# Decay matrix from ScalarE, gates straight from PSUM, and the carried state's product scaled in PSUM, in a Mamba-2 and attention block on one core

## The chip, the core and the metric

The kernel runs on one core of a Trainium2 chip. The metric is the device time of one launch, in microseconds (us). The engines are TensorE (PE: matrix products and transposes), VectorE (DVE), ScalarE (ACT: activation functions), GpSimd (POOL) and SyncE (SP, which here only issues the weights' transfers). Each works through its own queue in order, and they wait for each other by semaphores. PSUM is where TensorE writes; SBUF is the main on-chip memory.

## What is computed

A hybrid layer (gated Mamba-2 scan beside dilated attention, then a feed-forward part), followed by two further transformer layers, for 512 tokens of width 1024. The change touches the scan alone:

```python
# 32 heads of 64, 4 groups of 8 heads, state 128, chunks of Q = 128 tokens
a_cs = jnp.cumsum(a, axis=-1)
Lmat = jnp.exp(jnp.where(tri, a_cs[..., :, None] - a_cs[..., None, :], -jnp.inf))
CB = jnp.einsum('bclgn,bcsgn->bcgls', Cr, Br)
y_diag = jnp.einsum('bcgjls,bcsgjp->bclgjp', CB[:, :, :, None] * Lmat, xdt)
...                                     # states carried from chunk to chunk
y_off = jnp.einsum('bclgn,bcgjpn,bcgjl->bclgjp', Cr, prev_states, jnp.exp(a_cs))
y = ssd_chunked(xs, dt, A, Bm, Cm) + d_skip.astype(jnp.float32)[:, None] * xs
y = y.reshape(b, S, SSM_D_INNER) * jax.nn.silu(z.astype(jnp.float32))
# then an RMS norm over each group of 512 channels and the product with w_ssm_out
```

## The kernel before

Every large product is run in float32 as three products of split operands (high x high, low x high, high x low). Weights come in slabs of 256 rows by 256 columns: SyncE fetches them, GpSimd splits them (L563, L565), and TensorE uses them. A panel is 256 output columns, kept in two PSUM banks that two panels share by turns, so a panel can begin once the panel before the last is evicted (semaphore `evicted`).

The scan has 16 units u = 4g + c: group g of 8 heads, chunk c of 128 tokens. The list `SCAN`, written out by hand, fixes one order that every engine follows. Between panels (z: gates, xs: inputs of the next group, "so": output of the group before) it places the steps of the units:

- A(u): TensorE forms the scores of the chunk. VectorE subtracts the columns of the cumulated decay from its rows for 8 heads at once (L1537), takes the minimum with 0 (L1540), forms `xdt` and `xdd`, masks the scores (`cbm`), waits for ScalarE's exponential (L1141) and multiplies it into `M` (L1550). ScalarE then asks for the next unit's decay rows.
- Bp(u): TensorE multiplies `M` by `xdt` (L808), the old state by C (L813) and forms the chunk's addition to the state (L817). VectorE brings `state` up to date (L1558 to L1564) and builds `yb` (L1576 to L1584): skip term, decayed product of the old state (L1578), diagonal part, gate. ScalarE squares `yb` and takes the root (L1156, L1158).
- N(u): VectorE normalizes `yb` to `yn` (L1587, L1592). Cp(u): TensorE transposes `yn` (L822), ScalarE and VectorE split it into `yT_hi` and `yT_lo`.
- epi of a z panel: VectorE scales four blocks out of PSUM into `zbuf` (L1603), ScalarE takes Silu over all of it (L1126).
- xs panels: VectorE scales (cu, L1435) and does three of the four taps of the convolution (L1444), ScalarE the first tap and Silu (`xsf`, L1077), TensorE transposes it (xt, L788).

PSUM bank 0 of `AUX` serves the transposes, bank 1 scores and state, bank 2 the diagonal part, bank 3 the product of the old state.

Of the kernel before, what the change touches and what calls it, by code (L numbers as in the profile page):

```python
# [10 lines left out]
ACT = mybir.ActivationFunctionType  # L11
ALU = mybir.AluOpType
# [240 lines left out]
def build(nc, I, out):  # L253
    ctx = ExitStack()
    with ctx:
# [77 lines left out]
        yoffb = r.put("yoffb", [P, GW])  # L333
# [680 lines left out]
        def _(act):  # L1014
# [96 lines left out]
            def load_decay(u):  # L1111
                g, c = u // NB, u % NB
                load(acs_row[:, u % 2], bass.AP(tensor=acs_dram.tensor, offset=g * HG * S + c * P, ap=[[0, P], [S, HG], [1, P]]), acs_in[u % 2])
# [5 lines left out]
            act.wait_ge(sq_ready, DC)  # L1119
            load_decay(0)  # L1120
            load_gain(0)

            def silu_gate(g, panel):
                act.wait_ge(evicted, 2 * (PAN[("z", g)] + panel) + 2)
                part = zbuf[:, :, panel * PANEL:(panel + 1) * PANEL]
                A(part, part, ACT.Silu).then_inc(z_ready, 1)  # L1126

            def scan_step(tok):
# [9 lines left out]
                elif kind == "A":  # L1138
                    act.wait_ge(acs_in[u % 2], 16 * (u // 2 + 1))
                    act.wait_ge(decay_step, 2 * u + 2)  # L1140
                    A(M[:, u % 2], M[:, u % 2], ACT.Exp).then_inc(decay_exp, 1)  # L1141
                    A(etot[:, u % 2, :], acs_row[:, u % 2, :, P - 1], ACT.Exp).then_inc(decay_exp, 1)
                    if u < 15:
                        if u:
                            act.wait_ge(decay_step, 2 * u)
                            act.wait_ge(decay_exp, 2 * u)
                        load_decay(u + 1)
# [213 lines left out]
        def _(dve):  # L1361
# [154 lines left out]
            def heads(ap):  # L1516
                return ap.rearrange("p (h d) -> p h d", d=HD)
# [6 lines left out]
            def scan_step(tok):  # L1524
# [6 lines left out]
                elif kind == "A":  # L1531

                    dve.wait_ge(acs_in[u % 2], 16 * (u // 2 + 1))
                    if u == 0:
                        dve.wait_ge(tokc_ready, 2)
                    wait(dve, ydiag_done, u - 1)
                    V.tensor_tensor(M[:, u % 2], acs_row[:, u % 2], tokc[:, c, 1, hs].unsqueeze(2).broadcast_to([P, HG, P]),  # L1537
                                    ALU.subtract).then_inc(decay_step, 1)
                    dve.wait_ge(decay_step, 2 * u + 1)
                    V.tensor_scalar(M[:, u % 2], M[:, u % 2], 0.0, None, ALU.min).then_inc(decay_step, 1)  # L1540
# [10 lines left out]
                elif kind == "Bp":  # L1551
# [25 lines left out]
                    if c:  # L1577
                        step(V.tensor_tensor(heads(yoffb[:]), heads(AUX[:, 3, :]), spread(tokc[:, c, 3, hs]), ALU.mult))  # L1578
                    dve.wait_ge(ydiag_done, u + 1)
                    step(V.tensor_tensor(yb[:], yb[:], AUX[:, 2, :], ALU.add))  # L1580
                    if c:
                        step(V.tensor_tensor(yb[:], yb[:], yoffb[:], ALU.add))
                    dve.wait_ge(z_ready, 2 * g + 2)
# [14 lines left out]

            def gate_panel(key, panel):
                done(key, panel)  # L1600
                g = key[1]
                for t in range(NB):
                    ins = V.tensor_scalar(zbuf[:, t, panel * PANEL:(panel + 1) * PANEL], psum_tm(key, panel)[:, t, :], rstd_col[:, t:t + 1], None, ALU.mult)  # L1603
                    if t % 2:
                        ins.then_inc(evicted, 1)
# [49 lines left out]
            for tok in SCAN:  # L1655
                if tok[0] == "epi":
                    key, panel = tok[1], tok[2]
                    if key[0] == "z":
                        gate_panel(key, panel)
                    elif key[0] == "xs":  # L1660
                        conv_panel(key, panel, 8 + 4 * key[1] + 2 * panel)
                    elif key[0] == "so":
                        add_scan_out(key, panel)
                    else:
                        qkv1(key)
                elif tok[0] != "mm":
                    scan_step(tok)
# [389 lines left out]
```

## Time and profile before

| | |
|---|---|
| median of 3 runs | 2751.45 us (2749.63 to 2753.14) |
| the profiled execution's own time | 2752.16 us |
| its span in the profile | 2750.4 us |
| mean granted TensorE clock | 0.969 of full speed |
| TensorE products | busy 2591.3 us (94%) |
| VectorE / ScalarE / GpSimd | busy 1463.7 / 705.3 / 1609.5 us |
| the chain that ended last, by engine | PE 72%, DVE 7%, issue 2%, ACT 1% |

The span is divided by stages in the trace: the scan lies between about 110 and 530 us. A row of a timeline gives the start and the length of an instruction, the engine, the line of the kernel, output <- input, the shape, and in brackets how long the engine had been idle before it and whose work ended that. Idle time of an engine that nobody waits for costs nothing. The granted clock is TensorE's: 1.00 is 2.4 GHz, 0.50 is 1.2 GHz.

### The profile page before, as it was taken

How to read it: one execution, taken by the hardware profiler on the slowest of the kernel's cores; microseconds unless marked ns; L12 is line 12 of the kernel's file. 1: busy time of each engine (PE TensorE's matmuls, PEld its weight loads, DVE VectorE, ACT ScalarE, POOL GpSimd, SP SyncE). 2: the span in 40 equal slices, each digit the busy share in tenths (PEclk: the TensorE clock that was granted, in tenths of full speed). 3: DMA queues.
4: the chain of work that ended last, by engine and by line, in shares of the span. 5: the costliest groups of instructions: out<-in, count | busy, mean ns of one | idle time of the engine just before them, and what ended most of it. 6: DMA issues, size and time to landing. Idle time of an engine off the chain costs nothing.

```text
span 2750.4 us, 37333 instructions
## 1 busy us (share of the span) xinstructions
PE 2591.3 (94%) x12895; PEld 2117.8 (77%) x12895; DVE 1463.7 (53%) x2056; ACT 705.3 (26%) x1251; POOL 1609.5 (59%) x1548
## 2 busy tenths in 40 slices
PE   8889899898999999999999889999999998999998
PEld 6768777787877778888777667888867776788886
DVE  6676676453433533330357757876145445688722
ACT  2233333100123221110224433432012222343300
POOL 5534454474444667777644346888754332588874
PEclk9988898999999999999999999999999999999999
DMA  4332232232222333333321122333322221233331
GB/s 139 121 84 81 69 100 81 66 99 65 66 65 59 108 88 97 97 96 97 92 91 61 48 58 73 96 95 99 96 62 84 68 77 35 70 98 97 95 99 63
DMA packets 235781, 229.17 MB, mean 83 GB/s; under 512 B 15808, under 2 KB 228288, under 8 KB 235664
## 3 DMA queue, kind: packets, MB, share of 16 engines
q1 hardware_dynamic: 212224, 204.72, 25.6%
q10 hardware_dynamic: 23440, 22.82, 2.9%
q8 instruction: 82, 1.34, 0.2%
q14 instruction: 35, 0.29, 0.0%
HBM read 222.67 MB, written 4.82 MB: 83 GB/s over the span
## 4 chain that ended last, share of the span: by engine, by line
PE 72%; DVE 7%; issue 2%; ACT 1%; DVEq 0%; ACTq 0%
PE PS L605 56%; PE PS L599 5%; PE PS L676 2%; PE AUX L904 1%; PE AUX L853 1%; PE AUX L953 1%; PE AUX L943 1%; DVE opA_lo L1378 1%; DVE AUX L1849 1%; DVE half_acc L1396 1%; PE AUX L958 1%; PE AUX L872 1%; PE AUX L701 0%; DVE bstat L1932 0%; PE AUX L862 0%
## 5 line engine op out<-in xcount | busy, mean ns | idle before, releaser
L563 POOL TENSOR_SCALAR whi<-raw 128x512 fp32r<-128x512 f32 x772 | 554.4, 718 | 1048.9 <-issue 522.1
L565 POOL TENSOR_TENSOR wlo<-raw,whi 128x512 fp32r<-128x512 f32 x772 | 1056.4, 1368 | 64.5
L605 PE MATMUL PS<-opA_hi,whi 128*128 128x512 f32 x1872 | 749.9, 401 | 18.4 <-DVE opA_lo L1378 6.9
L605 PE MATMUL PS<-opA_lo,whi 128*128 128x512 f32 x1872 | 735.5, 393 | 0.0
L605 PE MATMUL PS<-opA_hi,wlo 128*128 128x512 f32 x1872 | 735.4, 393 | 0.0
L605 PEld LDWEIGHTS PS<-opA_hi,whi 128*128 128x128 f32 x1872 | 356.2, 190 | 105.2 <-issue 12.5
L605 PEld LDWEIGHTS PS<-opA_hi,wlo 128*128 128x128 f32 x1872 | 355.4, 190 | 76.5
L605 PEld LDWEIGHTS PS<-opA_lo,whi 128*128 128x128 f32 x1872 | 356.3, 190 | 71.8 <-issue 1.0
L1873 DVE SCALAR_TENSOR_TENSOR facc<-fu,vec,facc 128x512 f32<-128x512 f32 x176 | 202.2, 1205 | 52.7 <-ACT facc L1267 52.7
L599 PE MATMUL PS<-whi,opA_hi 128*128 128x256 f32 x704 | 210.4, 299 | 1.4 <-DVE y_ssm L1614 1.0
L599 PE MATMUL PS<-whi,opA_lo 128*128 128x256 f32 x704 | 203.0, 288 | 0.0
L599 PE MATMUL PS<-wlo,opA_hi 128*128 128x256 f32 x704 | 202.8, 288 | 0.0
L605 PE MATMUL PS<-hid_hi,whi 128*128 128x512 f32 x480 | 186.7, 389 | 0.0
L605 PE MATMUL PS<-hid_lo,whi 128*128 128x512 f32 x480 | 186.7, 389 | 0.0
L605 PE MATMUL PS<-hid_hi,wlo 128*128 128x512 f32 x480 | 186.7, 389 | 0.0
L599 PEld LDWEIGHTS PS<-whi,opA_hi 128*128 128x128 f32 x704 | 139.4, 198 | 10.0 <-issue 5.3
L599 PEld LDWEIGHTS PS<-whi,opA_lo 128*128 128x128 f32 x704 | 139.3, 198 | 2.1 <-issue 2.0
L599 PEld LDWEIGHTS PS<-wlo,opA_hi 128*128 128x128 f32 x704 | 138.8, 197 | 0.0
L1831 DVE COPY branch<-PS 128x512 f32<-128x512 f32 x32 | 21.0, 687 | 219.5 <-PE PS L605 160.2
L1295 ACT ACTIVATE sc<-sc,bstat 128x128 f32<-128x128 f32 (+3 forms) x128 | 70.8, 554 | 188.9 <-DVE bstat L1934 188.9
L605 PEld LDWEIGHTS PS<-hid_hi,wlo 128*128 128x128 f32 x480 | 90.1, 188 | 18.8
L605 PEld LDWEIGHTS PS<-hid_lo,whi 128*128 128x128 f32 x480 | 90.1, 188 | 18.8
(302 smaller groups left out, 3534.0 us busy)
## 6 DMA issues: line engine op xcount, KB each, us to landing
raw<-in_w_in_dram SPq DMA_DIRECT2D x184, 256.0 KB, 2.8
raw<-in_ffn_w_in_dram SPq DMA_DIRECT2D x176, 256.0 KB, 2.7
raw<-in_ffn_w_out_dram SPq DMA_DIRECT2D x88, 256.0 KB, 2.7
raw<-in_a_w_qkv_dram SPq DMA_DIRECT2D x48, 256.0 KB, 2.7
raw<-in_w_ffn_gate_dram SPq DMA_DIRECT2D x44, 256.0 KB, 2.7
raw<-in_w_ffn_up_dram SPq DMA_DIRECT2D x44, 256.0 KB, 2.7
raw<-in_w_ffn_down_dram SPq DMA_DIRECT2D x44, 256.0 KB, 2.7
acs_row<-acs_dram ACTq DMA_DIRECT2D x16, 512.0 KB, 5.6
```

What stands on the lines that cost most here:

```text
L563: nc.gpsimd.tensor_scalar(whi[slot][:], raw[raw_slot][:], 1.0, 1.0, ALU.mult, ALU.mult).then_inc(w_high, 1)
L565: nc.gpsimd.tensor_tensor(wlo[slot][:], raw[raw_slot][:], whi[slot][:].bitcast(F32), ALU.subtract).then_inc(slab_split, 1)
L599: last = nc.tensor.matmul(psum_tm(key, panel)[:, t, :], a, b[:, c, :], start=t % 2 == 0 and k + n == 0, stop=k == total - 1 and n == 2, sk ...
L605: last = nc.tensor.matmul(psum_fm(key, panel, m), a, b[:, k, :], start=k + n == 0, stop=k == total - 1 and n == 2)
L676: last = nc.tensor.matmul(psum_fm(key, panel, m), a, b[:, n0, :], start=n0 + n == 0, stop=n0 == SLAB * nk - 1 and n == 2)
L853: nc.tensor.matmul(AUX[:, bank, 0:width], q1[j][:, 2 * gi + hh, q0:q0 + P], k1[j][:, 2 * gi + hh, k0:k0 + width], start=True, stop=False)
L872: last = nc.tensor.matmul(AUX[:, 2, 0:P], probT[:, n, :], v1[j][:, b, gi * PANEL + hh * P:gi * PANEL + (hh + 1) * P], start=n == 0, stop=n ...
L904: last = nc.tensor.matmul(AUX[:, e, 0:width], q2[j % 2][rows, hh, q0:q0 + P], k2[j % 2][rows, hh, 0:width], start=True, stop=True)
L943: last = nc.tensor.transpose(AUX[:, 2 + e, b * P:(b + 1) * P], src, ident[:])
L953: last = nc.tensor.matmul(AUX[:, 2, e * 64:e * 64 + 64], pT[:, e, b, :], v2[j % 2][:, b, hh * P + e * 64:hh * P + e * 64 + 64], start=b == ...
L1295: A(sc[:, u % 2, e, 0:width], sc[:, u % 2, e, 0:width], ACT.Exp, bias=bstat[:, u % 4, 2 + e:3 + e], accum_out=bstat[:, u % 4, 4 + e:5 + e] ...
L1873: V.scalar_tensor_tensor(facc[:, j, :], fu[:, j, tap:tap + S], col("ffn_conv_w_2", 132 * l + 44 * tap + FT * half + m + 2 * i), facc[:, j, ...
```

## The change

There are three edits. ScalarE forms the argument of the decay exponential itself, one Relu for each head: `Relu(column - row)` with the column as a bias per partition, and the exponential is taken with scale -1. ScalarE also takes Silu of the gates straight from PSUM, with the token's factor as a scale per partition; VectorE waits for it and passes the eviction on. The decayed product of the old state is written back into its PSUM bank, and `yoffb` goes.

```diff
             act.wait_ge(sq_ready, DC)
+            act.wait_ge(tokc_ready, 2)
...
             def silu_gate(g, panel):
-                act.wait_ge(evicted, 2 * (PAN[("z", g)] + panel) + 2)
-                part = zbuf[:, :, panel * PANEL:(panel + 1) * PANEL]
-                A(part, part, ACT.Silu).then_inc(z_ready, 1)
+                key = ("z", g)
+                act.wait_ge(slab_done, slab_end(key, panel))
+                if g:
+                    act.wait_ge(y_step, YSTEPS[4 * g])
+                for t in range(NB):
+                    A(zbuf[:, t, panel * PANEL:(panel + 1) * PANEL], psum_tm(key, panel)[:, t, :], ACT.Silu,
+                      scale=rstd_col[:, t:t + 1]).then_inc(z_ready, 1)
...
                 elif kind == "A":
+                    g, c = u // NB, u % NB
                     act.wait_ge(acs_in[u % 2], 16 * (u // 2 + 1))
-                    act.wait_ge(decay_step, 2 * u + 2)
-                    A(M[:, u % 2], M[:, u % 2], ACT.Exp).then_inc(decay_exp, 1)
+                    wait(act, ydiag_done, u - 1)
+                    for h in range(HG):
+                        A(M[:, u % 2, h, :], acs_row[:, u % 2, h, :], ACT.Relu, bias=tokc[:, c, 1, g * HG + h:g * HG + h + 1],
+                          scale=-1.0).then_inc(decay_step, 1)
+                    act.wait_ge(decay_step, HG * (u + 1))
+                    A(M[:, u % 2], M[:, u % 2], ACT.Exp, scale=-1.0).then_inc(decay_exp, 1)
                     A(etot[:, u % 2, :], acs_row[:, u % 2, :, P - 1], ACT.Exp).then_inc(decay_exp, 1)
                     if u < 15:
-                        if u:
-                            act.wait_ge(decay_step, 2 * u)
-                            act.wait_ge(decay_exp, 2 * u)
+                        wait(act, decay_exp, 2 * u)
                         load_decay(u + 1)
...
                 elif kind == "A":
 
-                    dve.wait_ge(acs_in[u % 2], 16 * (u // 2 + 1))
                     if u == 0:
                         dve.wait_ge(tokc_ready, 2)
                     wait(dve, ydiag_done, u - 1)
-                    V.tensor_tensor(M[:, u % 2], acs_row[:, u % 2], tokc[:, c, 1, hs].unsqueeze(2).broadcast_to([P, HG, P]),
-                                    ALU.subtract).then_inc(decay_step, 1)
-                    dve.wait_ge(decay_step, 2 * u + 1)
-                    V.tensor_scalar(M[:, u % 2], M[:, u % 2], 0.0, None, ALU.min).then_inc(decay_step, 1)
...
-                        step(V.tensor_tensor(heads(yoffb[:]), heads(AUX[:, 3, :]), spread(tokc[:, c, 3, hs]), ALU.mult))
+                        step(V.tensor_tensor(heads(AUX[:, 3, :]), heads(AUX[:, 3, :]), spread(tokc[:, c, 3, hs]), ALU.mult))
...
-                        step(V.tensor_tensor(yb[:], yb[:], yoffb[:], ALU.add))
-                    dve.wait_ge(z_ready, 2 * g + 2)
+                        step(V.tensor_tensor(yb[:], yb[:], AUX[:, 3, :], ALU.add))
+                    dve.wait_ge(z_ready, 8 * g + 8)
...
                     if key[0] == "z":
-                        gate_panel(key, panel)
+                        dve.wait_ge(z_ready, 8 * key[1] + 4 * panel + 4)
+                        dve.sem_inc(evicted, 2)
```

On ScalarE, from Bp(0) to A(2) in the first group, the order before is this (the first row squares `yb`, `M` is the decay matrix, the last row asks for the next unit's rows):

```order
L1156 ACTIVATE yt,ystat<-yb 128x512 [waits y_step]
L1158 ACT_TABLE_LOAD
L1158 ACTIVATE ystat<-ystat 128x1 [waits y_stat]
L1141 ACT_TABLE_LOAD [waits decay_step]
L1141 ACTIVATE M<-M 128x1024 [waits acs_in0]
L1142 ACTIVATE etot<-acs_row 128x8
L1021 DMA acs_row<-acs_dram 128x8x128 [waits decay_exp,decay_step]
```

And this is the same place of ScalarE's queue after the change (line numbers are those of the changed kernel):

```order
L1163 ACTIVATE yt,ystat<-yb 128x512 [waits y_step]
L1165 ACT_TABLE_LOAD
L1165 ACTIVATE ystat<-ystat 128x1 [waits y_stat]
L1147 ACTIVATE M<-acs_row,tokc 128x128 [waits ydiag_done,acs_in0]
L1147 ACTIVATE M<-acs_row,tokc 128x128 x7
L1150 ACT_TABLE_LOAD
L1150 ACTIVATE M<-M 128x1024 [waits decay_step]
L1151 ACTIVATE etot<-acs_row 128x8
L1020 DMA acs_row<-acs_dram 128x8x128 [waits decay_exp]
```

Eight Relu stand ahead of the table load, which no longer waits for VectorE; the number of table loads is the same.

On VectorE, from A(1) of the first group to the first `yb`, the order before:

```order
L1537 TENSOR_TENSOR M<-acs_row,tokc 128x1024 [waits acs_in1]
L1540 TENSOR_SCALAR M<-M 128x1024 [waits decay_step]
L1543 TENSOR_TENSOR xdt<-xs_tok,tokc 128x512 [waits aux0_read]
L1545 TENSOR_TENSOR xdd<-xs_tok,tokc 128x512
L1547 TENSOR_TENSOR cbm<-AUX,tri 128x128 [waits aux1_done]
L1550 TENSOR_TENSOR M<-M,cbm 128x1024 [waits decay_exp,aux1_read]
L1603 TENSOR_SCALAR zbuf<-PS,rstd_col 128x256 [waits slab_done]
L1603 TENSOR_SCALAR zbuf<-PS,rstd_col 128x256 x3
L1564 COPY state<-AUX 128x512 [waits aux1_done,decay_exp]
L1576 TENSOR_TENSOR yb<-xs_tok,dsk 128x512 [waits state_step]
```

And the same stretch of VectorE after the change:

```order
L1545 TENSOR_TENSOR xdt<-xs_tok,tokc 128x512 [waits z_ready,aux0_read]
L1547 TENSOR_TENSOR xdd<-xs_tok,tokc 128x512
L1549 TENSOR_TENSOR cbm<-AUX,tri 128x128 [waits aux1_done]
L1552 TENSOR_TENSOR M<-M,cbm 128x1024 [waits decay_exp,aux1_read]
L1566 COPY state<-AUX 128x512 [waits z_ready,aux1_done,decay_exp]
L1578 TENSOR_TENSOR yb<-xs_tok,dsk 128x512 [waits state_step]
```

The two rows on `M` and the four copies are gone, and `xdt` and `state` carry the wait for the gates (`z_ready`) instead.

## Rows read from the trace of the kernel before

**Rows 1.** Windows: us, busy (x instructions) of each engine, granted clock, DMA share, GB/s.

```profile
110.00:530.00 420.00, 366.96 (x2065) 316.92 (x2064) 287.53 (x364) 141.94 (x199) 201.06 (x184) 0.90 0.30 82
...
182.00:188.00 6.00, 6.00 (x18) 3.93 (x18) 1.38 (x2) 0.01 (x1) 0.00 (x0) 0.50 0.01 3
```

**Rows 2.** TensorE's timeline: start, us, what, [idle before, who ended it].

```profile
154.60 0.80 PE L798 MATMUL AUX<-bcf 128*128 128x128 f32 x2 [2.91 <-DVE state L1564]
...
156.86 3.43 PE L808 MATMUL AUX<-xdt,M 128*128 128x64 f32 x15 [1.47 <-DVE yb L1584]
...
180.72 0.66 PE L822 MATMUL AUX<-ident,yn 128*128 128x128 f32 x4 [4.38 <-DVE yn L1592]
...
277.12 0.53 PE L605 MATMUL PS<-opA_hi,whi 128*128 128x512 f32 x1 [1.03 <-DVE y_ssm L1612]
...
436.69 0.63 PE L788 MATMUL AUX<-ident,xsf 128*128 128x128 f32 x4 [2.42 <-DVE yT_lo L1596]
...
496.07 1.11 PE L822 MATMUL AUX<-ident,yn 128*128 128x128 f32 x4 [3.61 <-DVE yn L1592]
```

**Rows 3.** Timelines of ScalarE and VectorE, and the page's row on the decay rows' DMA.

```profile
138.78 0.37 ACTq L1021 DMA_DIRECT2D acs_row<-acs_dram  x1
...
153.98 1.06 ACT L1126 ACTIVATE zbuf<-zbuf 128x1024 f32<-128x1024 f32 x1 [2.72 <-DVE zbuf L1603]
...
156.75 0.63 ACT L1156 ACTIVATE yt<-yb 128x512 f32<-128x512 f32 x1 [1.71 <-DVE yb L1584]
...
158.78 0.20 ACT L1158 ACTIVATE ystat<-ystat 128x1 f32<-128x1 f32 x1
...
170.70 0.58 ACT L1164 ACTIVATE yT_hi<-AUX 128x512 fp32r<-128x512 f32 x1
...
260.28 0.20 ACT L1158 ACTIVATE ystat<-ystat 128x1 f32<-128x1 f32 x1
...
161.48 1.23 DVE L1550 TENSOR_TENSOR M<-M,cbm 128x1024 f32<-128x1024 f32 x1 [1.38 <-ACT etot L1142]
...
177.77 2.04 DVE L1550 TENSOR_TENSOR M<-M,cbm 128x1024 f32<-128x1024 f32 x1 [0.66 <-ACT etot L1142]
...
265.34 1.94 DVE L1550 TENSOR_TENSOR M<-M,cbm 128x1024 f32<-128x1024 f32 x1
...
273.01 1.03 DVE L1582 TENSOR_TENSOR yb<-yb,yoffb 128x512 f32<-128x512 f32 x1
...
acs_row<-acs_dram ACTq DMA_DIRECT2D x16, 512.0 KB, 5.6
```

**Rows 4.** ScalarE's groups (count, busy us, mean ns, idle before), and a pair.

```profile
L1295 ACT ACTIVATE sc<-sc,bstat 128x128 f32<-128x128 f32 x32 | 12.5, 394 | 40.1 <-DVE bstat L1934 40.1
...
L1205 ACT ACTIVATE prob<-AUX,astat 128x256 f32<-128x256 f32 x12 | 5.6, 465 | 0.0
...
L1141 ACT ACT_TABLE_LOAD x16 | 20.5, 1283 | 39.5 <-DVE M L1540 39.5
...
L1141 ACT ACTIVATE M<-M 128x1024 f32<-128x1024 f32 x16 | 17.0, 1060 | 0.2
...
L1069 ACT ACTIVATE cacc<-cu,vec 128x512 f32<-128x512 f32 x24 | 18.2, 804 | 36.1 <-DVE cu L1435 36.1
...
300.29 1.51 ACT L1069 ACTIVATE cacc<-cu,vec 128x512 f32<-128x512 f32 x2
```

**Rows 5.** VectorE's groups by form.

```profile
L1537 DVE TENSOR_TENSOR M<-acs_row,tokc 128x1024 f32<-128x1024 f32 x16 | 23.4, 1463 | 0.0
...
L1540 DVE TENSOR_SCALAR M<-M 128x1024 f32<-128x1024 f32 x16 | 13.0, 812 | 0.5
...
L1603 DVE TENSOR_SCALAR zbuf<-PS,rstd_col 128x256 f32<-128x256 f32 x32 | 13.2, 471 | 0.0
...
L1578 DVE TENSOR_TENSOR yoffb<-AUX,tokc 128x512 f32<-128x512 f32 x12 | 8.3, 691 | 0.4
...
L1849 DVE TENSOR_TENSOR AUX<-branch,AUX 128x512 f32<-128x512 f32 x32 | 22.0, 686 | 5.8 <-PE AUX L707 5.8
```

More of the change, by code:

```diff
@@ L332, in build @@
         yt = r.put("yt", [P, GW])
-        yoffb = r.put("yoffb", [P, GW])
         yn = r.put("yn", [P, 3, GW])
@@ L1597, in scan_step @@
                                     ALU.subtract).then_inc(aux0_read, 1)
[L1599 to L1605, printed above, removed]
             def add_scan_out(key, panel):
```

## Prediction

> **What bounds the kernel now.** I read the windows first: the scan fills 110 to 530 us, and there TensorE is busy for 366.96 of 420 us at a mean granted clock of 0.90, VectorE for 287.53 and ScalarE for 141.94 [rows 1]. So TensorE bounds the kernel even here, and the change touches none of its instructions. What can be won is TensorE's idle time in the scan, and what its clock loses behind an idle stretch: between 182 and 188 us, right after a stall of 4.38 us, the clock was at half (0.50), so 6 us of products did the work of 3 [rows 1, 2].
>
> Next, TensorE's timeline, for the bracket of each row (idle time, and who ended it). The stalls to judge are these [rows 2]: 2.91 us before the score product of unit A(2), for the first copy into `state`; 1.47 us before Bp(1), for `yb`; 4.38 us before the transposes Cp(1), for `yn`; 1.03 us in group 1 before the panel xs, for the eviction of a "so" panel (groups 2 and 3 have the same one); 3.61 us before Cp(13), for `yn`. The others come from the convolution: TensorE's product for the old state, `yb`, the cu product, six tap steps, Silu, transpose (the 2.42 us at 436.69 is the last link of one [rows 2]). No instruction of the decay matrix or of the gates stands in those chains, so I leave them as they are.
>
> **The change part by part.**
>
> *Decay matrix.* VectorE loses 16 subtractions (23.4 us) and 16 minima (13.0 us), 1463 and 812 ns each [rows 5]. ScalarE gets 8 Relu of 128x128 with a bias per partition for each of 16 units. The nearest row is the exponential L1295, 128x128 with such a bias: 394 ns [rows 4]. Two instructions in a row overlap: two of 804 ns took 1.51 us together, so 0.10 us goes [rows 4]. Eight then take 8 x 0.30 + 0.1 = 2.5 us. Behind them stand the same table load (1.28) and the same exponential (1.06). From ScalarE being free to M being ready I get 2.5 + 1.28 + 1.06 + 0.05 = 4.9 us [rows 4]. Before, it was VectorE being free, plus subtraction and minimum, plus 2.4 us. The exponential waits for the eighth Relu, and the load of the next decay rows is queued behind it; it still goes out about when the table load starts, as before, so I charge nothing for it.
>
> The Trainium skill, "ScalarE: Activation LUTs", section "Rules for kernel authors", speaks against this part: it gives relu, min and add to VectorE. Its section "What ACT_TABLE_LOAD costs" has 186 ns plus 0.833 ns an element, 93 ns for each pointer operand and 93 ns of overlap, so an estimate of 2.4 us for the eight, which the rows bear out. The same section adds a drain of 1.38 us to a table switch. Here there is no room for it: from the start of Square (156.75) to that of the square root (158.78) 2.03 us pass, of which 0.63 are Square and 1.28 the load [rows 3, 4]. With it every M would be later by 1.4 us before as well as after, and the difference stays.
>
> *Gates.* VectorE loses 32 scaled copies of 471 ns (13.2 us in all), four for each of eight panels, so 13.2 / 8 = 1.65 us a panel [rows 5]. ScalarE's Silu of 128x1024 (1.06 us) becomes four of 128x256 from PSUM with a scale per partition: L1205, 128x256 out of PSUM with a bias, takes 465 ns [rows 4], so 4 x 0.365 + 0.1 = 1.5 us. The gate is ready 1.5 us behind the panel in place of 2.7, and the bank is free 1.5 in place of 1.65. The added wait stands in VectorE's queue with the next decay step and the eviction behind it. In the first group it ends before 152.3 us, worked out below; in the later ones VectorE has slack there.
>
> *Carried state's product.* The same two instructions of VectorE. Writing PSUM out of PSUM is L1849 in the trace: 686 ns, against 691 for the old L1578, so nothing [rows 5]. The sum behind it now has one operand in SBUF and one in PSUM, as L1849 has: 0.69 us. At 273.01 us, with both in SBUF, it took 1.03 [rows 3]. I take 0.35 us for each such step.
>
> *First group, A(1) to Bp(1).* ScalarE was ready for the Silu of z panel 1 with its table loaded at 153.98 - 2.72 = 151.26 us [rows 3]. Now A(1) must wait until its rows have landed (asked for at 138.78, 5.6 us to landing [rows 3]: 144.4), then 4.9 us: 149.3; 0.2 for the small exponential, 1.28 for the table, 1.5 for four Silu: 152.3 us. That is 1.5 us before VectorE was through with its copies (the Silu started on them at 153.98), so `state` is copied 1.5 us earlier, and `yb` is done at 155.2 in place of 156.7. TensorE's first two stalls lose 1.5 us.
>
> *A(2).* It gives that back. ScalarE takes 2.2 us from the start of Square (156.75) to the end of the square root (158.98) [rows 3]; now 155.2 to 157.4. Only then the Relu begin: 157.4 + 4.9 = 162.3 us, where the product started at 161.48 [rows 3]. N(0), the state and the panel xs come 0.8 us later than before, since VectorE used to form the decay beside that square root.
>
> *A(3) and Cp(1).* Here VectorE was slow: the product for M began at 177.77, 6.5 us after ScalarE had let go of yT_hi, and Cp(1) at 180.72 [rows 2, 3]. yT_hi was done at 170.70 + 0.58 = 171.3 us [rows 3]; now at 172.1. 172.1 + 4.9 = 177.0 us. The product M goes 0.8 us earlier; I take between nothing and 0.8 more, since its 2.04 us is a disturbed 1.2, so 1.2 us in the middle. **Term: 1.2 us.**
>
> *Groups 1 to 3, A(u+2).* Square root done at 260.28 + 0.20 = 260.5 us, + 4.9 = 265.4; the product M started at 265.34 [rows 3]. Even. Only the 0.35 us of the undisturbed sum shortens the way to the "so" eviction, out of a stall of 1.03: **3 x 0.35 = 1.05 us.** In group 3 the stall before Cp(13) gets besides the step A(15), where 0.25 us is won by the same count: **0.25 us.**
>
> **Sum.** 1.2 + 1.05 + 0.25 = 2.5 us. The profiled execution took 2752.16 us (span 2750.4): 2749.7. It lies 0.7 us above the median of 2751.45, so in the measure of the medians I predict 2749.0 us: 49.6 us less work on VectorE for 2.5 us.
>
> **Bounds.** A Relu: 0.13 apiece if it cost only an eighth of the exponential (1060 / 8), 0.39 without overlap [rows 4]. That moves M by -1.3 to +0.7 us, at five places on the path at most: -6.5 to +3.5 us. The PSUM write: -0.1 to +0.35 (as if it were disturbed like the old sum) for 12, +4 us at most.
>
> **Rivals.**
>
> *The clock stays up (0.30).* At 180.72 the stall shrinks from 4.38 us to between 2 and 2.8, since the panel ahead starts 0.8 later and `yn` comes 0.8 to 1.6 earlier. The stall of 2.42 us left the transposes behind it at 0.63 us for four, the 2.91 one slowed what followed (0.80 us for two) [rows 2]. Should it hold, the 6 us at 0.50 behind it become 3, and a few tenths on either side: 3.3 more, so 5.8 us in all, 2746.4 by the profiled execution, 2745.7 by the medians. For it: both ends of this stall draw closer. Against it: the upper end of my range is near the 2.91 us.
>
> *ScalarE becomes the bound at A(u+2) (0.14), slower.* Without VectorE's disturbances the old way from `yb` to M is shorter than 7.1 us, and mine has nothing to spare: 2.2 + 4.9. If the Relu come out at 0.39 or more, each M there is 0.7 us or more later, so are `yb` of Bp(u+1) and the "so" eviction, and the 1.03 us before the xs panel [rows 2] grows. It decides from about 1.9 us of delay, where that stall is as long as the 2.91 us one, behind which the products ran slow: 3 groups x (1.9 + 3.3) = 15.6 us, less 1.2: 2766 us. Below that it costs 3 x 0.7 = 2.1, and the sum is about 2752. For it: one queue now carries Square, root, Relu, table, exponential in series. Against it: rows 4 give 0.30.
>
> *Nothing moves (0.16).* TensorE's stalls end with the convolution's chains, the 1.5 us of the start go back at A(2), and the product M (1.23 to 2.04 us in rows 3) comes out long wherever it now lies: 2751.5 us. The Trainium skill, "SBUF — State Buffer", section "Who interferes with whom", says that a VectorE instruction with two SBUF inputs is blocked by a GpSimd one that reads SBUF. That agrees with the 1.03 us here, against 691 ns for the line with an operand in PSUM [rows 3, 5]. By it the product M, which keeps two such inputs, can lose what it won.
>
> **How the numbers follow.** Forecast 0.40, clock held 0.30, no movement 0.16, slower 0.14. What a measurement of this kernel can tell from no change is 0.2%, 5.5 us. The forecast (2.5) and no movement lie within it; of the clock case a little over four fifths lie beyond, as other stalls of the first group can add to it, and a tenth of the forecast; of the slower case some four fifths. Faster 0.29, same 0.59, slower 0.12. The range for 8 in 10 reaches past the clock case and takes in the small form of the slower one: 2742 to 2756 us.
>
> **What would show it.** Relu rows of 0.37 to 0.41 us starting 0.30 apart. M's product in A(2) starting about 6.2 us behind the first `yb`, against 4.8. The stall before Cp(1) at 2 to 3 us, and in the windows behind it 0.50 or not. The stalls for xsf at 4.4 us unchanged. The xs stall of 1.03 at 0.6 to 0.7. I am wrong if the stalls of the convolution's chains change, if a stall for ScalarE's Silu shows on TensorE, or if M is late in groups 1 to 3.

## The result

The changed kernel takes 2754.2 us (median of 20 executions, 2739.3 to 2757.2), the kernel before 2749.2 us beside it (20 executions, 2746.4 to 2753.1). The ratio is 1.0014, 95% interval [1.0008, 1.0021]: slower by 2 to 6 us, less than the 0.2% that the forecast counted as a difference, and in the range forecast, but on the wrong side of the forecast of 2.5 us less. By the medians it is 5.0 us, by the means of the 20 executions each 3.8.

Of the 20 executions of the changed kernel 17 took 2752 to 2757 us and three 2739 to 2746 us. The profiled one was one of the three: 2742.84 us, span 2741.0. A second trace of the same kernel (a_again below) is of the common kind: 2756.3 us, span 2754.5. I read the scan's steps in the first and the clock in both.

ScalarE's and VectorE's groups in the scan after the change (instructions, busy us, mean ns, idle before):

```profile
L1147 ACT ACTIVATE M<-acs_row,tokc 128x128 f32<-128x128 f32 x128 | 39.0, 390 | 0.0
...
L1129 ACT ACTIVATE zbuf<-PS,rstd_col 128x256 f32<-128x256 f32 x32 | 12.6, 476 | 0.1
...
L1580 DVE TENSOR_TENSOR AUX<-AUX,tokc 128x512 f32<-128x512 f32 x12 | 8.4, 699 | 0.4
...
L1582 DVE TENSOR_TENSOR yb<-yb,AUX 128x512 f32<-128x512 f32 x16 | 11.0, 687 | 0.6
```

The unit prices of the forecast hold: a Relu 390 ns and 39.0 / 128 = 0.30 us apiece (against 394 in [rows 4]), a gate 476 ns (465 forecast), the product written to PSUM 699 ns (691 before [rows 5]), the sum with one operand in PSUM 687 ns.

TensorE's timeline in the changed kernel, profiled execution (start, length, what, [idle before, who ended it]), against [rows 2]:

```profile
152.12 0.49 PE L797 MATMUL AUX<-bcf 128*128 128x128 f32 x2 [0.87 <-DVE state L1566]
...
154.38 1.97 PE L807 MATMUL AUX<-xdt,M 128*128 128x64 f32 x16 [1.78 <-DVE yb L1586]
...
163.48 1.12 PE L821 MATMUL AUX<-ident,yn 128*128 128x128 f32 x4 [3.80 <-DVE yn L1594]
...
272.57 0.50 PE L604 MATMUL PS<-opA_hi,whi 128*128 128x512 f32 x1 [0.72 <-DVE y_ssm L1606]
...
490.49 0.74 PE L821 MATMUL AUX<-ident,yn 128*128 128x128 f32 x4 [3.61 <-DVE yn L1594]
```

The 2.91 us for the first `state` are 0.87, the 1.47 for `yb` 1.78, and the 1.03 before the xs panel 0.72. The 4.38 us before Cp(1) are gone here, and 0.93 in the second trace. The 3.61 us before Cp(13) are unchanged. There is a new stall, 3.80 us before Cp(0) (2.61 in the second trace), for `yn` of unit 0. What it waits for stands in VectorE's timeline:

```profile
153.54 0.69 DVE L1586 TENSOR_TENSOR yb<-yb,zbuf 128x512 f32<-128x512 f32 x1
...
161.34 1.22 DVE L1552 TENSOR_TENSOR M<-M,cbm 128x1024 f32<-128x1024 f32 x1 [5.58 <-ACT etot L1151]
162.48 0.15 DVE L1589 RECIPROCAL ystat<-ystat 128x1 f32<-128x1 f32 x1
162.68 0.75 DVE L1594 SCALAR_TENSOR_TENSOR yn<-yb,ystat,gain 128x512 f32<-128x512 f32 x1
```

VectorE stands 5.58 us (1.38 before [rows 3]) at the product M of A(2), and N(0), whose `ystat` has long been there, is queued behind it. On ScalarE, Square starts at 154.27, and the Relu behind it:

```profile
154.27 0.63 ACT L1163 ACTIVATE yt<-yb 128x512 f32<-128x512 f32 x1 [3.12 <-DVE yb L1586]
...
156.30 0.20 ACT L1165 ACTIVATE ystat<-ystat 128x1 f32<-128x1 f32 x1
156.41 2.43 ACT L1147 ACTIVATE M<-acs_row,tokc 128x128 f32<-128x128 f32 x8
158.86 1.28 ACT L1150 ACT_TABLE_LOAD   x1
```

From Square to the product M it takes 161.34 - 154.27 = 7.07 us; before, 161.48 - 156.75 = 4.73 [rows 3].

### The profile page after: what moved, and what is told of

Read it like the earlier page. It is cut to its first block, busy times and chain, and to the rows that moved or that the text cites. A ratio compares the mean times of both kernels' runs of the same rounds, so it can differ in the third digit from the quotient of the medians.

```text
span 2741.0 us, 37402 instructions
## 1 busy us (share of the span) xinstructions
PE 2582.1 (94%) x12877; PEld 2113.3 (77%) x12895; DVE 1410.0 (51%) x1992; ACT 746.8 (27%) x1403; POOL 1608.4 (59%) x1548
## 4 chain that ended last, share of the span: by engine, by line
PE 83%; DVE 11%; issue 3%; ACT 3%; DMA 0%; ACTq 0%; DVEq 0%
PE PS L604 61%; PE PS L598 7%; PE PS L675 2%; DVE cacc L1451 2%; PE AUX L903 1%; PE AUX L952 1%; PE AUX L807 1%; PE AUX L852 1%; PE AUX L942 1%; DVE opA_lo L1385 1%; DVE AUX L1844 1%; DVE half_acc L1403 1%; PE AUX L957 1%; PE AUX L871 1%; PE AUX L787 1%
## 5 line engine op out<-in xcount | busy, mean ns | idle before, releaser
L604 PEld LDWEIGHTS PS<-hid_hi,whi 128*128 128x128 f32 x480 | 90.1, 188 | 18.6
```

The lines of the kernel that those rows point to most:

```text
L604: last = nc.tensor.matmul(psum_fm(key, panel, m), a, b[:, k, :], start=k + n == 0, stop=k == total - 1 and n == 2)
```

## Where the time went: one table

All traces were divided at the same instructions. Scan: first transpose of xs to the last product with `M` of a Bp. Gap: from there to the first score product of the first attention stage. att1: its first to last score product. Two stretches behind it are not in the table, since they hardly differ: 493.4 or 493.5 us to the first score product of the second layer's attention, and 214.4 or 214.5 us from there to the first copy of that attention's output product out of PSUM (`branch`; 215.1 us in p_psum). att2: from this copy to the last score product of the third layer, so the second layer's feed-forward part and most of the third layer's attention. Tail: the rest, up to the execution's time. The kernels of the experiments are described below: p_decay, p_gates and p_psum have one of the three edits, `all` has all of them, the number in _d8 or _d15 is that of the unread products put on TensorE, and hyb has the change in all units but one. The unread products are taken off the gap.

```
                  time   start  scan   gap   att1   att2   tail
before          2752.2   119.2  391.2  118.0  276.9  694.0  445.1
before_d15      2750.6   118.8  393.5  116.8  271.5  689.8  449.1
p_decay         2747.6   119.6  393.4  116.8  271.5  690.9  447.5
p_gates         2751.0   121.8  393.4  116.9  271.6  690.4  449.1
p_psum          2753.0   121.6  392.9  116.8  271.7  693.9  447.5
after           2742.8   118.7  386.5  116.8  271.5  692.3  449.1
a_again         2756.3   121.7  387.2  118.1  276.9  695.6  449.0
all             2753.1   118.0  387.4  118.1  276.9  695.8  449.0
after_d8        2747.0   120.7  387.4  118.2  271.4  692.3  447.5
after_d15       2754.6   119.9  387.3  118.2  273.7  695.4  449.1
hyb             2743.0   121.1  386.5  116.8  271.9  689.8  449.0
```

The scan is shorter in every trace of the changed kernel: five traces of the kernel before (with and without delay) have 390.4 to 393.5 us, mean 392.4; seven of the changed one 386.5 to 390.0, mean 387.6. So the scan gave 4.8 us, not 2.5. It was lost in stages that the diff does not touch: by the means of the same traces the gap took 0.7 us more, att1 0.2, att2 1.9 and the tail 0.9. Even the start, which lies ahead of the work that the diff touches, is between 117.8 and 121.8 us in the twenty traces.

The two windows that show how (us, busy and instructions of each engine, granted clock, DMA), first of the second trace of the changed kernel, then of the kernel before with 15 unread products:

```profile
505.00:545.00 40.00, 37.02 (x216) 32.65 (x215) 14.55 (x26) 5.61 (x10) 21.63 (x22) 0.91 0.30 80
625.00:905.00 280.00, 258.31 (x1388) 214.28 (x1387) 103.10 (x202) 58.75 (x120) 125.89 (x132) 0.96 0.24 63
```

```profile
505.00:545.00 40.00, 37.02 (x236) 33.36 (x235) 17.57 (x29) 5.62 (x10) 20.79 (x21) 0.96 0.27 73
625.00:905.00 280.00, 258.29 (x1432) 216.46 (x1431) 105.32 (x205) 58.75 (x120) 129.48 (x135) 0.98 0.25 65
```

TensorE is busy for the same 37.02 of 40 and 258.3 of 280 us, but the clock is 0.91 against 0.96 and 0.96 against 0.98. (The counts of its instructions are no measure of this: the profiled execution of the changed kernel has 207 in the first window, at 0.96.) Even the stalls are the same. The second stall of the first attention stage in the same two kernels, in that order:

```profile
668.23 1.65 PE L852 MATMUL AUX<-k,q 128*128 128x384 f32 x2 [2.28 <-DVE osb L1709]
```

```profile
672.80 0.91 PE L854 MATMUL AUX<-k,q 128*128 128x384 f32 x2 [2.28 <-DVE osb L1715]
```

The same idle time of 2.28 us for the same tile, and the pair of products behind it takes 1.65 us or 0.91.

## The experiments

The kernel before was timed beside every one of them: 2748.5 us in the first four, 2749.3 in the next four, 2748.3 with d4, d8, d12 of the changed kernel and d8 of the one before, 2750.0 with before_d4, before_d12 and hyb_d8, 2748.7 with the last three. Times are medians of 6 to 12 executions.

**The parts alone.** The first is the changed kernel once more; the next three are the kernel before with one edit each.

> The changed kernel again, for a trace of its usual kind (17 of its 20 runs took 2752 to 2757 us, 3 took 2739 to 2746, and the profiled one, 2742.8, was one of the three). Theory CLOCK (mine): the instruction times of the scan are the same in both kinds, and they part at the two short stalls of the first group (0.87 and 1.78 us before A(2) and Bp(1)): in the long kind the granted clock falls there or behind Cp(0), and at further places that the short kind is spared. Expect median 2754 and, in a long trace, at least 3 us more at half clock in the scan than the before trace. Rival LATE: the long kind has longer stalls for ScalarE or VectorE work at A(u+2) (M ready later than before), with the clock as before; then TensorE's idle time in the scan is over 55 us against 54 before and 51.5 in the short trace.

Measured: 2754.1 us, ratio 1.0012 [1.0002, 1.0023]. Neither theory holds: from 110 to 530 us the granted clock is 0.90, as in the kernel before, and TensorE is idle for 50.2 us there against 53.0. The scan is not where the time goes.

```profile
110.00:530.00 420.00, 369.79 (x2081) 319.11 (x2081) 235.32 (x303) 184.81 (x355) 194.14 (x184) 0.90 0.30 83
```

> Only ScalarE forms the decay argument; gates and carried product as before. Theory CLOCK: two kinds of runs as with the whole change if this edit carries it, since A(1) is early and A(2) late: median 2752 to 2756. Theory LATE: ScalarE's Relu chain is the whole loss: median 2754 or more, in one kind. If the gates carry it: 2749.

```diff
+                    for h in range(HG):
+                        A(M[:, u % 2, h, :], acs_row[:, u % 2, h, :], ACT.Relu, bias=tokc[:, c, 1, g * HG + h:g * HG + h + 1],
+                          scale=-1.0).then_inc(decay_step, 1)
...
-                    V.tensor_tensor(M[:, u % 2], acs_row[:, u % 2], tokc[:, c, 1, hs].unsqueeze(2).broadcast_to([P, HG, P]),
-                                    ALU.subtract).then_inc(decay_step, 1)
...
-                    V.tensor_scalar(M[:, u % 2], M[:, u % 2], 0.0, None, ALU.min).then_inc(decay_step, 1)
```

Measured: 2747.0 us, 0.9992 [0.9983, 1.0001]. Both theories (2752 us or more) missed.

> Only the gates go by ScalarE out of PSUM. The first state copy comes up to 1.5 us earlier, and A(2) stays on VectorE, so nothing gives it back. By my working 2748 (1.5 us less). If the earlier copy alone brings the clock to fall at Cp(0) or spares it, the runs are of two kinds; if the gates are a loss by the wait in VectorE's queue: 2750 or more.

```diff
-                A(part, part, ACT.Silu).then_inc(z_ready, 1)
...
+                for t in range(NB):
+                    A(zbuf[:, t, panel * PANEL:(panel + 1) * PANEL], psum_tm(key, panel)[:, t, :], ACT.Silu,
+                      scale=rstd_col[:, t:t + 1]).then_inc(z_ready, 1)
...
-                        gate_panel(key, panel)
+                        dve.wait_ge(z_ready, 8 * key[1] + 4 * panel + 4)
+                        dve.sem_inc(evicted, 2)
```

Measured: 2748.1 us, 0.9998 [0.9990, 1.0007].

> Only the carried product is scaled in PSUM. By my working 3 x 0.35 us less: 2748.2. Rival: a PSUM write that is slower in place than row L1849 says would make it 2750 to 2753.

```diff
-                        step(V.tensor_tensor(heads(yoffb[:]), heads(AUX[:, 3, :]), spread(tokc[:, c, 3, hs]), ALU.mult))
+                        step(V.tensor_tensor(heads(AUX[:, 3, :]), heads(AUX[:, 3, :]), spread(tokc[:, c, 3, hs]), ALU.mult))
...
-                        step(V.tensor_tensor(yb[:], yb[:], yoffb[:], ALU.add))
+                        step(V.tensor_tensor(yb[:], yb[:], AUX[:, 3, :], ALU.add))
```

Measured: 2746.6 us, 0.9990 [0.9981, 0.9999]. So no part is slower alone, and the three are 5 to 6 us slower together by the medians (3.6 to 3.8 by the means). The new stall belongs to the decay edit: alone it has it as well, 2.56 us before Cp(0), and the other two don't:

```profile
156.20 0.49 PE L798 MATMUL AUX<-bcf 128*128 128x128 f32 x2 [2.59 <-DVE state L1563]
...
167.56 1.07 PE L822 MATMUL AUX<-ident,yn 128*128 128x128 f32 x4 [2.56 <-DVE yn L1591]
...
182.95 0.66 PE L822 MATMUL AUX<-ident,yn 128*128 128x128 f32 x4 [1.63 <-DVE yn L1591]
```

**Is it the place of the tensors?** The change frees 2 KB of each partition, and the tensors behind it move.

> All three edits (decay matrix, gates, scaled product in PSUM) in one kernel, but the buffer that the third edit frees stays allocated, so that every tensor lies where it lay before. Theory 1, the three edits together bring the program to its first attention stage at an unlucky moment: same time as the changed kernel, 2753 to 2755 us, scan (first transposes of xs to last state product) 386 to 388 us, first attention stage 276.9 us. Theory 2, the loss comes from the 2 KB by which later tensors move: near the kernels with one edit, 2746 to 2748 us.

```diff
+        yoffb = r.put("yoffb", [P, GW])
```

Measured: 2754.1 us, 1.0013 [1.0004, 1.0022], scan 387.4, att1 276.9 us: the tensors' place is out.

**Is it the moment of arrival?** Products of the identity that nobody reads, 0.213 us each, stand ahead of the panels of the first attention stage, behind the scan and the stall of 2.98 us that follows it.

```diff
+            keep_warm(15)
             for key in QKV1(0)[2:]:
                 panel_mm(key, 0)
```

> The changed kernel with 15 products of the identity (0.213 us each, 3.2 us) put on TensorE between the last product of the scan and the first panel of the first attention stage; nothing reads them. Theory 1, the length of the stages behind the scan follows from when they start and from what TensorE did before: the stage turns from its long kind (276.9 us) to its short one (271.5 us), and the kernel is 1 to 3 us faster than the changed one (2751 to 2753 us) though it does 3.2 us more. Theory 2, later stages are as long whatever their start: 2757.4 us, 3.2 us above the changed kernel.

Measured: 2755.9 us, 1.0022 [1.0013, 1.0031]. Missed by 3 us: att1 had 273.7 us, and att2 stayed at 695.4.

> The kernel before with the same 15 products (3.2 us) at the same place. Theory 1: the time moves by another amount than 3.2 us, anywhere from -2 to +8 us; its profile of before had the long first attention stage (276.9 us), and with the short one it would be 2747 us. Theory 2: 3.2 us more, 2752 us.

Measured: 2751.0 us, 1.0009 [1.0000, 1.0018]. Within the first theory's wide range, and near the second. These two decided nothing. The same with fewer products did:

> The changed kernel with 4 unread products (0.213 us each, 0.85 us) on TensorE ahead of the panels of the first attention stage. Theory 1 (what the clock costs in a stage hangs on the moment at which TensorE's stalls fall, with nothing else changed): the time does not follow the delay; with 0.85 us the first stall of the attention stage comes between where the long kind was seen (clock low 9.9 us or more after the stall's end) and the short one (8.9 to 9.2 us), so either, 2750 to 2756 us. Theory 2 (a delay only adds itself): 2754.1 + 0.85 = 2755.0 us.

Measured: 2749.4 us, 0.9999 [0.9987, 1.0010]. Just under the first theory's range, and 5.6 us under the second.

> The same with 8 products, 1.7 us. Theory 1: this shift moves the clock's fall behind the first attention stall from 10.3 us after its end to about 8.6, where the short kind was seen: attention stage 271 to 273 us, 2754.1 + 1.7 - 4.5 = 2751 us, faster than the changed kernel although it does more. Theory 2: 2755.8 us.

Measured: 2747.0 us, 0.9994 [0.9985, 1.0003]; att1 271.4 us. (The times in these two expectations, 8.6 to 10.3 us behind a stall's end, are read with a wrong zero and some 11 us too large. By the trace's own zero the clock falls at the first stall of att1, of 5.23 us, 1.1 us before that stall's end in the second trace of the changed kernel, and 2.9 us before it with 8 products. The shift is the one expected.)

> The same with 12 products, 2.55 us. Theory 1: somewhere between the 1.7 us (about 2751) and the 3.2 us (measured, 2755.9): 2752 to 2756 us. Theory 2: 2756.7 us.

Measured: 2752.8 us, 1.0014 [1.0006, 1.0023].

> The kernel before with 8 products, 1.7 us. Theory 1: the kernel before usually meets the short attention stage, and can lose it by a shift of 1.7 us: 2749.3 + 1.7 = 2751 to 2756 us. Theory 2: 2751.0 us.

Measured: 2756.0 us, 1.0017 [1.0007, 1.0026].

1.7 us of useless work make the changed kernel 7 us faster and the kernel before 7 us slower (5.3 and 5.9 us by the means). The theory that a delay only adds itself forecast 2755.8 and 2751.0. The windows over the second stall of the first attention stage and behind it, of the second trace of the changed kernel and of the one with 8 products (their first score products start at 627.0 and 628.0 us):

```profile
655.00:670.00 15.00, 12.72 (x73) 10.63 (x72) 7.97 (x12) 0.60 (x1) 7.71 (x9) 0.94 0.33 87
670.00:685.00 15.00, 15.00 (x105) 13.57 (x105) 4.91 (x11) 2.21 (x6) 5.90 (x7) 0.95 0.14 36
```

```profile
655.00:670.00 15.00, 12.72 (x76) 10.68 (x75) 7.97 (x12) 0.60 (x1) 7.84 (x9) 1.00 0.35 87
670.00:685.00 15.00, 14.93 (x114) 14.10 (x112) 4.94 (x12) 2.22 (x6) 7.32 (x8) 1.00 0.22 53
```

TensorE is busy for 12.72 us in both windows of 655 to 670, and the clock falls in the one and holds in the other.

**What is the change worth with the arrival averaged out?** I completed the series for the kernel before.

> The kernel before with 4 unread products (0.85 us) ahead of the panels of the first attention stage. Theory 1 (arrival decides): anything from 2748 to 2756 us. Theory 2: 2750.1 us. Over the five shifts, less their own 0.213 us a product, the changed kernel has a mean of 2750.2; if its scan gain of 4 us or more counts once the arrival is averaged out, the kernel before has 2753 to 2755; if it does not, 2750.

Measured: 2751.1 us, 1.0005 [0.9996, 1.0014].

> The kernel before with 12 unread products (2.55 us). Theory 1: between the 1.7 us (2756.0) and the 3.2 us (2751.0): 2750 to 2757 us. Theory 2: 2751.8 us.

Measured: 2753.7 us, 1.0013 [1.0004, 1.0022].

**Undoing the late step.** In unit 2 alone VectorE forms the argument, beside ScalarE's square root, as before (`yoffb` stays allocated here, as in `all`):

```diff
+BYV = (2,)
...
-                    for h in range(HG):
+                    for h in range(HG if u not in BYV else 0):
...
-                    A(M[:, u % 2], M[:, u % 2], ACT.Exp, scale=-1.0).then_inc(decay_exp, 1)
+                    A(M[:, u % 2], M[:, u % 2], ACT.Exp, scale=1.0 if u in BYV else -1.0).then_inc(decay_exp, 1)
...
+                    if u in BYV:
...
+                        V.tensor_tensor(M[:, u % 2], acs_row[:, u % 2], tokc[:, c, 1, hs].unsqueeze(2).broadcast_to([P, HG, P]),
+                                        ALU.subtract).then_inc(decay_step, 1)
...
+                        V.tensor_scalar(M[:, u % 2], M[:, u % 2], 0.0, None, ALU.min).then_inc(decay_step, HG - 1)
```

> The whole change, but in unit 2 alone the decay argument is formed by VectorE as before (the pair of subtraction and minimum), since that unit's argument on ScalarE stood behind a table load and a full queue. Theory 1, the time hangs on the moment of arrival at later stages: the scan stays within 2 us of the changed kernel's 387, the time is that of one of two levels, 2747 or 2754 us. Theory 2, the loss sits in unit 2 (ScalarE late behind the gates): 2750 us or less, with a scan shorter by 2 us or more.

Measured: 2744.7 us, 0.9985 [0.9976, 0.9994]. The time is under both levels of the first theory and fits the second, but the scan (386.5 us) is only 0.7 to 0.9 us shorter than in most traces of the changed kernel, not 2, so neither holds in full. Its VectorE at that place:

```profile
155.92 0.69 DVE L1595 TENSOR_TENSOR yb<-yb,zbuf 128x512 f32<-128x512 f32 x1
156.65 1.23 DVE L1548 TENSOR_TENSOR M<-acs_row,tokc 128x1024 f32<-128x1024 f32 x1
157.98 0.69 DVE L1551 TENSOR_SCALAR M<-M 128x1024 f32<-128x1024 f32 x1
...
161.38 1.23 DVE L1561 TENSOR_TENSOR M<-M,cbm 128x1024 f32<-128x1024 f32 x1 [1.31 <-ACT etot L1153]
```

The product M starts 161.38 - 156.61 = 4.8 us behind `yb`, and the wait of Cp(0) for `yn` is 0.15 us in place of 3.80 and 2.61; before Cp(1) it waits for 2.04 us, in place of none and 0.93. Group 0 (from the first transpose of xs to the one that ends the first wait for the next group's xsf, mostly 4.4 us long) takes 78.4 us, against 81.3 in six of seven traces of the changed kernel (79.2 in the profiled one), and 84.3 in three of the five of the kernel before (82.0 and 82.5 in the others). Was it lucky with its arrival?

> The whole change with unit 2's decay argument on VectorE, and 8 unread products (1.7 us). If its 2744.7 us is a lucky arrival, it loses it by this shift: 2750 to 2756 us. If that version is fast for its own sake: 2746.4 us or less.

Measured: 2742.8 us, 0.9972 [0.9960, 0.9984].

> The whole change with unit 2's decay argument on VectorE, and 4 unread products (0.85 us). If the version is fast at any arrival: 2742 to 2747 us. If it was lucky twice: 2748 to 2756 us.

Measured: 2742.8 us, 0.9980 [0.9970, 0.9990].

> The same with 12 products (2.55 us). Fast at any arrival: 2743 to 2748 us. Lucky twice: 2750 to 2757 us.

Measured: 2745.2 us, 0.9988 [0.9979, 0.9997].

> The same with 15 products (3.2 us). Fast at any arrival: 2744 to 2749 us. Lucky twice: 2750 to 2757 us. The mean over its five shifts, less the products' own time: 2743 to 2745 us if it is fast for its own sake, 2748 to 2751 us if it is as the other two.

Measured: 2746.4 us, 0.9992 [0.9982, 1.0003]. The medians less the products' own time:

```
products          0       4       8      12      15    mean
before       2749.2  2750.2  2754.3  2751.1  2747.8  2750.5
changed      2754.2  2748.5  2745.3  2750.3  2752.7  2750.2
unit 2 kept  2744.7  2741.9  2741.0  2742.6  2743.2  2742.7
```

Averaged over five arrivals the whole change is worth 0.3 us. With spreads of 2.5 and 3.5 us in the rows, such a difference of means is uncertain by some 4 us (twice the root of 2.5²/5 + 3.5²/5), so the scan's 4.8 us lie at the edge of what it allows: whether they count in full stays undecided. The version that keeps unit 2 on VectorE beats both kernels at all five, by 7.8 us and 7.5 us in the mean. Most of that is not the undone step: its five traces have a mean scan of 385.9 us, 1.7 less than the changed kernel, and are 1.0 us shorter in the gap, 0.9 in att1, 2.8 in att2 and 1.2 in the tail, where the work is the same. Group 0 gave 2.9 us, and 1.2 of them went again behind it. So that this version is fast at these five arrivals is measured; why the stages behind its scan are short at nearly all of them is not shown.

## Why the prediction was wrong

*Unit prices, A(1), the sum in PSUM: right.* Relu at 0.30, Silu, PSUM write and the 0.35 us of the sum came as worked out. The 1.03 us before the panel xs are 0.72, which is 0.31 of the 0.35. `state` came earlier by more than I had: the stall lost 2.0 us and not 1.5. (My own count gives 153.98 - 152.3 = 1.7; the 1.5 was a slip.) In groups 1 to 3 A(u+2) was to be even, and is: from the square root's end to the product M 261.08 - 256.23 = 4.85 us, before 4.86 [rows 3]:

```profile
256.03 0.20 ACT L1165 ACTIVATE ystat<-ystat 128x1 f32<-128x1 f32 x1
...
261.08 1.65 DVE L1552 TENSOR_TENSOR M<-M,cbm 128x1024 f32<-128x1024 f32 x1 [3.77 <-ACT etot L1151]
```

*A(2): the time right, what stands behind it missed.* I had M's product 162.3 - 155.2 = 7.1 us behind `yb`; it came 161.34 - 154.23 = 7.1 us behind it. But I charged it 0.8 us, the product's own shift, and wrote that N(0) "come 0.8 us later". N(0) is queued behind that product, and Cp(0), which had not waited before, waits 2.5 to 3.8 us for it. Keeping unit 2 on VectorE gives 2.9 us back in group 0. What was won at the start made it visible, since TensorE now reached Cp(0) sooner, and the stall mostly takes that back: counted from the first transpose of xs, Cp(0) starts at 43.5 to 44.7 us in the five traces of the kernel before, at 44.8 in three of the changed one and at 46.2 or 46.3 in four, and at 42.4 to 44.0 with unit 2 kept. (The list of signs has 6.2 us behind `yb` for this product, which doesn't follow from the working's 7.1.)

*A(3) and Cp(1): right direction, too small.* 4.38 us became 0.93 or less in these two traces (1.63 in two others), not 2 to 2.8. Cp(0)'s new stall had already moved TensorE back: in the five traces with unit 2 kept, where Cp(0) waits 0.4 us at most, the stall before Cp(1) is 2.04 to 2.09 us, as forecast.

*Cp(13): the 0.25 us did not come.* The product of A(15) did start 0.31 us sooner behind the square root (5.32 us for 5.63), but the stall is 3.61 us in every trace.

*The scan's sum: 2.5 us forecast, 4.8 measured* (392.4 - 387.6). Group 0 gave 84.3 - 81.3 = 3.0 us in the commonest traces, 2.5 in the mean. Behind it both kernels come in variants 2 us apart: the last stretch, from the last wait of 4.4 us for xsf, takes 97.0 to 97.2 us where the next wait for xsf is 2.3 to 2.4 us long, and 98.8 to 99.5 where that is 2.9 to 3.3. The first is so in one of five traces of the kernel before and in five of seven of the changed one. That is 1.3 of the 4.8 us in the mean, more of it clock than stall.

*The step that failed:* the one that I never wrote down as a step, "TensorE bounds the kernel", so the whole sum was the scan's and everything behind it was carried over unchanged (2752.16 - 2.5). The stages behind the scan are unchanged in work, but not in time: gap and att1 take 118.1 + 276.9 = 395.0 us in the usual execution of the changed kernel and 116.8 + 271.5 = 388.3 in others, 6.7 us with TensorE's stalls the same but for 0.2 us (24.7 and 24.9 in all). att2 adds 689.8 to 695.8. So the term that I had at nothing, everything behind the scan, is worth more either way than the sum. My rival "the clock stays up" looked at this for one stall in the scan, and nowhere else. The "ScalarE becomes the bound" rival was near with the mechanism (ScalarE's series of work at A(u+2)), but it struck at unit 2 alone and not in groups 1 to 3.

That the moment of arrival decides is shown by the delays (7 us either way for 1.7 us), and the twenty traces show what it is that the work arrives at: a fall of the granted clock that keeps its own time. At Cp(13) and again at the next long stall, 2.98 us in all traces and just behind the scan, the clock falls, 30.7 us apart in every trace, though the ends of the two stalls lie 30.9 to 31.2 us apart. At the second of them the traces are in order:

- The clock fell 0.63 to 0.81 us before the stall's end in six traces (14 products of 0.43 us at half clock behind it in the second trace of the changed kernel); there the gap is 118.0 to 118.2 us. In the other fourteen it fell between 0.58 us before the end and 0.42 us behind it and stayed down half as long (7 such products in the profiled execution), and the gap is 116.7 to 116.9 us.
- At the first stall of att1, 5.23 us in all, the clock fell 0.8 to 1.4 us before the end in six traces (before, before_d8, a_again, all, after_d15, hyb_d12). In these alone it fell again at the stall of 2.28 us, and att1 is 273.7 to 276.9 us. Where it fell 2.0 us or more before the end, or 0.5 us or less, it did not, and att1 is 270.6 to 271.9.

Two windows of the same length, 3.8 us behind the end of the stall of 2.98 us, in the changed kernel's profiled execution and in its second trace:

```profile
525.50:527.50 2.00, 2.00 (x10) 1.63 (x9) 0.00 (x0) 0.00 (x0) 0.92 (x2) 1.00 0.00 0
```

```profile
529.30:531.30 2.00, 2.00 (x6) 1.52 (x6) 0.00 (x0) 0.00 (x0) 0.15 (x1) 0.50 0.00 0
```

The Trainium skill, "TensorE: Matmul & The Clock Gate", section "Part 1: The HAM clock gate (the "warmup" mystery)", says that what steers the clock is free-running and does not reset when a kernel starts. The traces agree: the clock's first fall comes anywhere from 35.6 to 38.5 us into the program, with the same work ahead of it. What one might expect from that, that the whole times come at random, they don't show: 17 of 20 executions of the changed kernel were of one kind.

*att2.* Here the clock's moment goes with a stall. The clock falls some 29 us behind the copy that opens the stretch. Where that is 29.1 to 29.25 us (nine traces), TensorE waits for VectorE's `opA_lo` at the first products of the feed-forward part, and is idle for 5.5 or 5.6 us up to that part's output; where it is 29.25 to 29.3 us (`all` and before_d4), for 3.6 us without that wait; where it is 29.4 to 29.8 (nine), for 2.9 or 3.0 us. In the second trace of the changed kernel:

```profile
1665.03 0.47 PE L604 MATMUL PS<-opA_hi,whi 128*128 128x512 f32 x1 [2.09 <-DVE opA_lo L1385]
```

The way to that output takes 317.7 to 317.9, 315.8 and 313.0 to 314.7 us accordingly, for the same work. By what steps the earlier fall makes that wait no run shows.

*Open.* Why the changed kernel's executions fall on the unlucky arrival so regularly, and why att2 takes 695.4 us or more in five of its seven traces and in none of the other kernels, even with the arrival shifted. Four of the five have the stall above, but so have traces of the others with 693.7 to 694.1 us.

## What to carry to other kernels

In this kernel, bound by TensorE and 2750 us long, a gain of a few microseconds in one stage is below what its other stages move by when they start a microsecond earlier or later. Test such a change at several arrivals, by a few unread products between the stages, and take the mean; one median can come out on either side, as here: 5.0 us slower with no products, 9.0 us faster with 8 in both kernels. And when an engine gets a longer series of work, look at what is queued behind the instruction that waits for it, not at that instruction's own shift.

## What the hardware did that I had not expected

- A stall of 2.28 us with the same work around it left the clock up (two products in 0.91 us) or let it fall (1.65 us; six of twenty traces), by when it came.
- 15 unread products (3.2 us) changed the time by 1.7 us in both kernels, 8 of them (1.7 us) by -7 and +7 us: more delay isn't more effect.
